# First stage of a two-block transformer kernel: late modulation sums dealt anew, modulation units in pairs, columns by transposes, latent queries rotated first

## The reference, cut to what matters

```
mod   = silu(c)     @ w_ada + b_ada      # 6 parts of 2048 columns: sh_a, sc_a, gt_a, sh_f, sc_f, gt_f
mod_c = silu(c_ctx) @ w_ada + b_ada      # only sh_a, sc_a are used
h  = rms_norm(x)   * (1 + sc_a)  + sh_a  # 256 latent tokens
hc = rms_norm(ctx) * (1 + csc_a) + csh_a # 256 context tokens
h @ w_in, hc @ w_in                      # 4928 columns, feeding four kinds of attention
```

## Time and profile before

| | us |
|---|---|
| median of 3 runs | 2803.4 (2800.49 to 2805.45) |
| the profiled execution | 2806.29 |
| its span | 2804.3 |
| PE busy | 2735.3 (98%) |
| DVE busy | 1696.7 (61%) |
| ACT busy | 1165.0 (42%) |
| POOL busy | 197.2 (7%) |
| DMA read over the span | 205 GB/s |

### The profile page before, as it was taken

The page is one execution under the profiler, slowest core; times in us unless marked ns, Lnnn a source line. Parts: engine busy times, 40 slices in busy tenths (PEclk is TensorE's granted clock), DMA queues, the critical chain, the costliest instruction groups (busy, mean ns, idle before and its releaser), DMA issues.

```text
span 2804.3 us, 32889 instructions
## 1 busy us (share of the span) xinstructions
PE 2735.3 (98%) x12547; PEld 2224.0 (79%) x12547; DVE 1696.7 (61%) x2039; ACT 1165.0 (42%) x1520; POOL 197.2 (7%) x219
## 2 busy tenths in 40 slices
PE   5999999999999999999999999999999999999998
PEld 2587877687888888888888888888888888888887
DVE  2378974766466666655574566554565655656566
ACT  3222224544444444444454444444444443444444
POOL 0024404101000000000040000000000000000000
PEclk9999999999999999999999999999999999999999
DMA  9988873246666677555555544655565656556563
GB/s 346 346 278 306 305 281 113 76 180 207 212 209 226 239 245 245 195 185 192 180 210 195 169 146 139 222 195 195 180 196 192 188 189 194 180 184 192 192 194 120
DMA packets 285788, 577.48 MB, mean 206 GB/s; under 512 B 13986, under 2 KB 18562, under 8 KB 283646
## 3 DMA queue, kind: packets, MB, share of 16 engines
q1 hardware_dynamic: 276936, 542.05, 57.9%
q0 software_dynamic: 6752, 31.14, 3.1%
q10 hardware_dynamic: 2006, 3.02, 0.3%
HBM read 571.04 MB, written 5.14 MB: 205 GB/s over the span
## 4 chain that ended last, share of the span: by engine, by line
PE 87%; issue 4%; DVE 4%; DMA 3%; POOL 1%; POOLq 1%; ACT 0%; DVEq 0%; SPq 0%; ACTq 0%
PE bank L384 27%; PE bank L386 26%; PE bank L385 26%; DMA w_raw<-in_w_ada 3%; PE bank L2021 1%; DVE proj_x L1677 1%; PE bank L667 1%; DVE w_lo L380 1%; PE bank L984 1%; PE bank L488 1%; PE bank L831 0%; PE bank L693 0%; PE bank L868 0%; PE bank L616 0%; PE bank L669 0%
## 5 line engine op out<-in xcount | busy, mean ns | idle before, releaser
L380 DVE TENSOR_TENSOR w_lo<-w_raw,w_hi 128x1024 fp32r<-128x1024 f32 (+1 forms) x848 | 1030.8, 1237 | 568.3 <-ACT w_hi L372 566.3
L372 ACT ACTIVATE w_hi<-w_raw 128x1024 fp32r<-128x1024 f32 (+1 forms) x848 | 880.9, 1054 | 1158.3 <-PE bank L386 994.1
L384 PE MATMUL bank<-w_hi,xa_hi 128*128 128x512 f32 (+1 forms) x2272 | 894.4, 394 | 10.0 <-DVE w_lo L380 10.0
L386 PE MATMUL bank<-w_hi,xa_lo 128*128 128x512 f32 (+1 forms) x2272 | 884.7, 389 | 0.0
L385 PE MATMUL bank<-w_lo,xa_hi 128*128 128x512 f32 (+1 forms) x2272 | 884.5, 389 | 0.0
L384 PEld LDWEIGHTS bank<-w_hi,xa_hi 128*128 128x128 f32 x2272 | 428.6, 189 | 109.8 <-issue 19.9
L386 PEld LDWEIGHTS bank<-w_hi,xa_lo 128*128 128x128 f32 x2272 | 428.2, 188 | 89.1
L385 PEld LDWEIGHTS bank<-w_lo,xa_hi 128*128 128x128 f32 x2272 | 428.6, 189 | 86.0
L384 PE MATMUL bank<-w_hi,ffn_act_hi 128*128 128x512 f32 x800 | 311.4, 389 | 0.0
L386 PE MATMUL bank<-w_hi,ffn_act_lo 128*128 128x512 f32 x800 | 311.3, 389 | 0.0
L385 PE MATMUL bank<-w_lo,ffn_act_hi 128*128 128x512 f32 x800 | 311.2, 389 | 0.0
(11 more groups left out here) (321 smaller groups left out, 1816.7 us busy)
## 6 DMA issues: line engine op xcount, KB each, us to landing
w_raw<-in_w_in SPq DMA_DIRECT2D x116, 1024.0 KB, 5.1
w_raw<-in_w_ada SPq DMA_DIRECT2D x80, 1024.0 KB, 7.3
w_raw<-in_w_up SPq DMA_DIRECT2D x64, 1024.0 KB, 5.7
w_raw<-in_w_down SPq DMA_DIRECT2D x64, 1024.0 KB, 5.0
w_raw<-in_ffn_wg SPq DMA_DIRECT2D x44, 1024.0 KB, 5.2
w_raw<-in_ffn_wu SPq DMA_DIRECT2D x44, 1024.0 KB, 5.2
w_raw<-in_ffn_wd SPq DMA_DIRECT2D x44, 1024.0 KB, 5.1
w_raw<-in_w_out SPq DMA_DIRECT2D x32, 1024.0 KB, 5.1
```

Source lines behind the costliest of these rows:

```text
L372: act.activation(whi[:, slot, ks, 0:w], raw[:, q, ks, 0:w], ACT.Copy)\
L380: dve.tensor_tensor(wlo[:, slot, ks, 0:w], raw[:, q, ks, 0:w], whi[:, slot, ks, 0:w].bitcast(F32), ALU.subtract).then_inc(sem("lo_made"), 1)
L384: pe.matmul(out, xh, wh, start=first, stop=False)
L386: return pe.matmul(out, xl, wh, start=False, stop=last)
```

## The change

- SP's five small loads at the start (c, c_ctx, g_attn, b_ada, identity) move to ACT's queue.
- Four late tiles, `LATE_AHEAD` (sums 2 and 3, k = 0 and 1), are loaded at the end of `FRONT` and summed by DVE right behind the last `h_lo`; the other 44 are dealt anew by `BY_VECTOR`, sums 4v+2 and 4v+3 ahead of 4v and 4v+1.
- At i = 1 DVE makes the sums before the two copies.
- The rows of b_ada for the late parts are loaded from ACT's queue in groups 1 and 2 of the front, instead of from SP behind the fourth load of the mixed stage.
- In the front, modulation units run in pairs with the pieces behind each pair; a chunk's columns come behind the pieces; columns are four transposes, and DVE reduces them.
- The folds of v = 0 and 1 come one unit later than the old rule would put them.
- POOL rotates the latent queries between the two halves of the grouped queries; the first copies into `probsT` wait for the second half.

```diff
-U_OUT = U_MIX + 4 * (len(WIN) - 2) + 4 * N_LATE_D + 4
+U_OUT = U_MIX + 4 * (len(WIN) - 2) + 4 * N_LATE_D
+LATE_AHEAD = [(2, 0), (3, 0), (2, 1), (3, 1)]
 def front_loads():
-    return loads
+    return loads + [("late", a, k) for a, k in LATE_AHEAD]
-BY_VECTOR = {2: (0, 2, 2, 4), 3: (0, 2, 0, 2), 4: (2, 2, 2, 2), 5: (2, 2, 2, 2), 6: (2, 2, 2, 4), 7: (4, 2, 4, 0)}
+BY_VECTOR = {2: (2, 2, 2, 2), 3: (0, 2, 0, 0), 4: (2, 2, 4, 2), 5: (2, 2, 2, 2), 6: (2, 2, 4, 2), 7: (2, 2, 2, 0)}
-    queue = [(a + s, k) for a in range(0, N_LATE_D, 2) for k in range(4) for s in range(2)]
+    queue = [(a + s, k) for v in range(3) for a in (4 * v + 2, 4 * v) for k in range(4) for s in range(2)]
+    queue = [tile for tile in queue if tile not in LATE_AHEAD]
-FOLD_AT = [min(i for i, n in enumerate(W) if n > LAST_SUM[v] and MIX[n][2] >= 1) for v in range(3)]
+FOLD_AT = [min(i for i, n in enumerate(W) if W[i - (v < 2)] > LAST_SUM[v] and MIX[n][2] >= 1) for v in range(3)]
 def front_read(sp, n):
+                elif kind == "late":
+                    sp.wait_ge(sem("sum_step"), 8 * q + 8)
 # act, where the first pair of probabilities is copied; dve the same
+                if s["d"] == 0:
+                    act.wait_ge(sem("rotated_pe"), 2)
 # sync: the five small loads leave, to the head of the scalar engine's program
-            sp.dma_start(crow[0:16, :], ...)
...
-                if n == 3:
-                    late_b_piece(0)
-                    late_b_piece(1)
 # scalar, in the loop over g
+                if g in (1, 2):
+                    for b in range(4):
+                        col = 2 * D + (4 * (g - 1) + b) * NCH
+                        act.dma_start(late_rows[g - 1][32 * b:32 * b + 32, :], ...)
 # vector: take(c)
-                cols = ps[4 + c % 2][:, 0:8].rearrange("p (k v) -> p k v", v=2)
+                cols = ps[4 + c % 2][:, :].rearrange("p (k j v r) -> p k v r j", k=4, j=4, v=2)[:, :, :, 0, :]
+                dve.tensor_reduce((s_col if c % 2 == 0 else b_col)[:, k, :], cols, AX.X, ALU.add)
+                dve.drain()
 # vector, behind the loop over g
+            multiply_ahead(0)
+            multiply_ahead(1)
+            def late_pairs(i):
+                for first in range(W[i] + 1, W[i] + 1 + FOLLOW[i], 2):
+                    multiply((first, first + 1))
 # vector, the loop over W
                 if i == 1:
+                    late_pairs(i)
                     win_copy(0)
                     win_copy(1)
+                    continue
                 if i >= 2:
                     behind(i - 2)
-                for first in range(n + 1, n + 1 + FOLLOW[i], 2):
-                    multiply((first, first + 1))
+                late_pairs(i)
 # tensor: columns(c)
-                    m = pe.matmul(ps[4 + c % 2][:, 2 * k:2 * k + 2], rows_1[:, c % 2, k * P:k * P + P], pick[:, :], ...)
+                    m = pe.transpose(ps[4 + c % 2][:, k * P:k * P + P], rows_1[:, c % 2, k * P:k * P + P], ident[:, :])
 # tensor: the loop over g
-                rest = list(PIECES[g])
-                for u in range(8):
-                    c, q = 2 * g + 2 + u // 4, u % 4
-                    ada_unit(c, q)
-                    if u < 5:
-                        w, j = rest.pop(0)
-                        early_piece(pe, w, g, j)
-                    if q == 3:
-                        columns(c)
-                for w, j in rest:
+                c = 2 * g + 2
+                for u in range(0, 8, 2):
+                    ada_unit(c + u // 4, u % 4)
+                    ada_unit(c + u // 4, u % 4 + 1)
+                    for w, j in (PIECES[g][0:2], PIECES[g][2:4], PIECES[g][4:5], PIECES[g][5:6])[u // 2]:
+                        early_piece(pe, w, g, j)
+                    if u % 4 == 2:
+                        columns(c + u // 4)
+                for w, j in PIECES[g][6:8]:
                     early_piece(pe, w, g, j)
 # gpsimd
             copied(8)
-            for i in range(2):
-                (norm and rope of the grouped queries of token tile i)
+            gqa_queries(0)
             (wait for mla_copied; rope of the latent queries)
             pool.drain().then_inc(sem("rotated_pe"), 1)
+            gqa_queries(1)
+            pool.drain().then_inc(sem("rotated_pe"), 1)
```

More of the change, by code:

```diff
@@ L413, in early_hi, with early_lo @@
                     .then_inc(sem("early_hi"), 1)
-        def early_lo(dve, w, g):
+        def early_lo(dve, w, g, halves=(0, 1)):
             q = FRONT.index(("win", w, g)) % 4
-            for h in range(2):
+            for h in halves:
                 dve.wait_ge(sem("early_hi"), 4 * g + (1 if w == 1 else 3) + h)
@@ L817, in att1_dve @@
                 wait(dve, "att_out", s["d"] - 1)
+                if s["d"] == 0:
+                    dve.wait_ge(sem("rotated_pe"), 2)
                 pt_copy(dve.tensor_copy, s, 1).then_inc(sem("att_pt_copied_d"), 1)
@@ L1296, in _ @@
         def _(sp):
[L1297 to L1302, removed]
             for i in range(4):
@@ L1313, in _ @@
                 front_read(sp, n)
-                src = w_ada_v[:, q, :, ada_cols(c)] if kind == "ada" else w_in_v[:, q, :, WIN[c][0]:WIN[c][0] + NCH]
+                if kind == "late":
+                    src = w_ada_v[:, q, :, 2 * D + c * NCH:2 * D + (c + 1) * NCH]
+                else:
+                    src = w_ada_v[:, q, :, ada_cols(c)] if kind == "ada" else w_in_v[:, q, :, WIN[c][0]:WIN[c][0] + NCH]
                 sp.dma_start(raw[:, n % 4, :, :], src).then_inc(sem(f"landed{n % 4}"), 16)
@@ L1389, in _ @@
         def _(act):
+            act.dma_start(crow[0:16, :], t["c"].rearrange("a (k p) -> (a k) p", p=P)).then_inc(sem("c_loaded"), 16)
+            act.dma_start(crow[16:32, :], t["c_ctx"].rearrange("(k p) -> k p", p=P)).then_inc(sem("c_loaded"), 16)
+            act.dma_start(csig[32:48, :], t["g_attn"].rearrange("a (k p) -> (a k) p", p=P)).then_inc(sem("consts_loaded"), 16)
+            act.dma_start(csig[48:80, :], t["b_ada"][:, 0:2 * D].rearrange("a (k p) -> (a k) p", p=P))\
+                .then_inc(sem("consts_loaded"), 16)
+            act.dma_start(ident[:, :], t["identity"]).then_inc(sem("consts_loaded"), 16)
             act.wait_ge(sem("memsets"), 2)
@@ L1421, in _ @@
                 h_hi(act, g, 1)
+                if g in (1, 2):
+                    for b in range(4):
+                        col = 2 * D + (4 * (g - 1) + b) * NCH
+                        act.dma_start(late_rows[g - 1][32 * b:32 * b + 32, :],
+                                      t["b_ada"][:, col:col + NCH].to_broadcast([32, NCH])).then_inc(sem(f"b_loaded{g - 1}"), 16)
             def win_copy(c):
@@ L1636, in _ @@
             dve.drain()
-            dve.scalar_tensor_tensor(g_one_b[:, :], small_cols[:, 2, :], 1.0, small_cols[:, 0, :], ALU.add, ALU.mult)
-            dve.tensor_reduce(pick[:, :], ident[:, :].rearrange("p (j v r) -> p v r j", j=4, v=2)[:, :, 0, :], AX.X, ALU.add).then_inc(sem("c_spread"), 1)
+            dve.scalar_tensor_tensor(g_one_b[:, :], small_cols[:, 2, :], 1.0, small_cols[:, 0, :], ALU.add, ALU.mult)\
+                .then_inc(sem("c_spread"), 1)
             def spread2(cols):
@@ L1684, in multiply, with multiply_ahead @@
                             reached[c] = ("lo_made", 2 * u + 2)
+            def multiply_ahead(k):
+                for j in range(KQ):
+                    for a in (2, 3):
+                        n = FRONT.index(("late", a, k))
+                        if j == 0:
+                            dve.wait_ge(sem(f"landed{n % 4}"), 16 * (n // 4) + 16)
+                        w, cj, acc = raw[:, n % 4, j, :], ccol[:, 4 * k + j:4 * k + j + 1], late_sums(a)
+                        if k == 0 and j == 0:
+                            m = dve.tensor_scalar(acc, w, cj, None, ALU.mult)
+                        else:
+                            dve.wait_ge(sem("sum_step"), reached[a][1])
+                            m = dve.scalar_tensor_tensor(acc, w, cj, acc, ALU.mult, ALU.add)
+                        m.then_inc(sem("sum_step"), 1)
+                        steps[0] += 1
+                        reached[a] = ("sum_step", steps[0])
             def add_rows(v):
@@ L2028, in columns @@
                 for k in range(4):
-                    m = pe.matmul(ps[4 + c % 2][:, 2 * k:2 * k + 2], rows_1[:, c % 2, k * P:k * P + P], pick[:, :],
-                                  start=True, stop=True)
+                    m = pe.transpose(ps[4 + c % 2][:, k * P:k * P + P], rows_1[:, c % 2, k * P:k * P + P], ident[:, :])
                 m.then_inc(sem("ada_columns"), 1)
@@ L2310, in _ @@
                      sin128[:, i, :], 64, 4)
+            copied(8)
+            gqa_queries(0)
             pool.wait_ge(sem("mla_copied_a"), 1)
```

9 lines of the change are left out of this document (4 added, 5 removed).

## The result

The changed kernel takes 2810.2 us (median of 22 runs, 2806.5 to 2812.7) against 2804.3 (22 runs, 2800.5 to 2808.7): a ratio of 1.0018, 95% interval 1.0011 to 1.0024. It is slower, by 5.9 us in the medians (5 us by the ratio), where 0.9 us less was forecast. The forecast time, 2802.5, is 7.7 us too low; the range (2793 to 2811) holds the result. What follows compares places in the traces.

What follows compares the result with a forecast made beforehand. PE was taken to bound the kernel nearly everywhere. Terms -2.5+17.6+1.9-10.8-3.7-3.4 = -0.9 took the profiled 2806.3 to 2805.4 us, and 2.9 less for the median gave 2802.5; range 2793 to 2811.

Steps and rivals of the forecast that it cites:

- The front: Stage up to 158.04 us: start, columns, groups and end together -2.5 us, with three groups of 29.3 us counted +0.5.
- L+13.5: Front's ring: second projection tile is free 13.5 us after L, the last modulation tile's landing; before it was 11.9.
- The start: Kernel start: first x load leaves at 0.74 instead of 3.05, so -2.3 us; bounds 0 and -2.3.
- Columns by transposes: Front: four transposes replace eight selector instructions, DVE reduces more; net -0.25 us on the path per chunk.
- The end of the front: From the start of the last columns to the front's end: 24.2 us instead of 25.5, so -1.3.
- The new wait: Before PE's first mixed-stage unit: idle 17.6 us for DVE's copy of projection 0, plus 1.9 of low clock.
- T+31.1: Mixed stage: DVE's copy of projection 0 is done 31.1 us after T, the end of the last h_lo.
- The mixed stage: Behind the new wait: PE's idle times before projections 3 and 4 and last fold go, -10.8 us, and -3.7 of clock.
- The queries: Near 462 us: POOL's flag comes earlier, 1.90 us idle and 1.5 of low clock go, -3.4.
- (a): Rival: bias-row spread eats the lead, PE waits before projection 3 again, +6.5+2.0, total 2811 us; chance 0.23.
- (b): Rival: stall only 12.3 us and the ring does not bind, groups of 27.8 us, total 2793; chance 0.19.
- (c): Rival: copy of projection 0 does not hold PE, so no stall, 17.6+1.9 go, total 2783 us; chance 0.05.

Runs made afterwards that it cites:

- e1: Changed kernel with the front's modulation units and pieces in the order of before, columns still by transposes; 2805.4 us.
- g3: Kernel before with small loads on ACT's queue, columns by transposes, latent queries first, plus the change's pairs; 2804.7 us.
- f3: Kernel before with the small loads on ACT's queue, columns by transposes and latent queries first; 2799.9 us.
- f4: Kernel before with the columns by transposes only; 2804.4 us.
- e4: Kernel before with only the latent queries rotated between the halves of the grouped queries; 2802.9 us.
- f1: Changed kernel with the old unit order and, on both engines, each early projection copied behind its own unit, ahead of that unit's sums; 2800.8 us.
- g2: Kernel of f1 with another deal of the late tiles (BY_VECTOR), projections 2 to 7; 2795.9 us (7 runs).
- e2: Changed kernel, units in pairs, with the odd chunk's columns ahead of the piece; 2805.1 us.
- f2: Kernel of f1 with two late tiles fewer behind projection 2's first unit and two more behind projection 5's third; 2799.1 us.

## Why the prediction was wrong, point by point

- **The front, the step that failed** ("Start, groups and end: -2.3-0.25+0.5-1.3", rounded to -2.5): it came as +0.6. The loop through the ring was seen, but the old loop was said to lie "under PE's own 28 to 29", so that pairs would cost 0.5 us in all. They cost 4.8 (e1, g3).
  - *The new loop's size.* "L+13.5" for the second projection tile was right: in the group of the rows above the last unit of the group before (the second of the two at 98.60) starts at 99.53 and the split is done at 110.54 + 2.36 = 112.90, 13.4 later. The next load into that buffer is used at 118.12, 5.2 later, as priced. The "four more at 2.7 us each" then took until 130.34, 12.2 us instead of 10.8: the first two behind the hold came 3.4 us apart. With that a group is 13.4 + 5.2 + 12.2 = 30.8, not 29.3. From last unit to last unit the three groups take 28.5 (40.67 to 69.13), 30.4 and 30.8 us: the first is as long as in the old order, as no piece stands ahead of the columns at 42.45 that open it.
  - *The old loop's size.* 28.5 (f3, f4), not 27.8; PE waits 1.2 to 1.3 us there for the last load of the last two groups. The mean of 29.3 in before hides three unequal groups, 28.7, 31.1 and 28.1 us, as two rows of before show beside the 44.68 and 132.53 of the earlier trace rows. In the second, 3.3 us were lost to a low clock at 73 to 81 us (0.57), which other executions have less of (e4: 0.79). At full clock PE and the ring were level, so PE's own saving could win nothing, and 29.3 as the measure of "nothing changes" was a poor base.

```profile
73.34 1.49 PE L2029 MATMUL bank<-row_pick,ada_rows 128*128 128x2 f32 x8 [0.72 <-ACT ada_rows L1407]
104.44 1.05 PE L2029 MATMUL bank<-row_pick,ada_rows 128*128 128x2 f32 x8 [0.72 <-ACT ada_rows L1407]
```

  - *The piece counted once too few.* The groups were priced from landing to landing, and the end from the start of the last columns. The step between them, from 1.8 to 3.9 us because the piece stands there, is in neither: +2.1.
- **The start, -2.3:** the first modulation product comes at 21.84 instead of 23.06, -1.2, though SP's first x load does leave at 0.74. The ten kernels with the small loads on ACT's queue have it at 20.9 to 22.0, mean 21.4, the three with them on SP's (before, e4, f4) at 22.4 to 23.1, mean 22.8: -1.5. By the first odd columns the gain is larger, 1.8 us (means of 42.6 and 44.3), and 2.2 in the two traces compared. The far end of 0 and -2.3 was chosen, and the truth lay between, near that end for the sum. Why the first load comes only half as much earlier was not tried.
- **Columns by transposes, -0.25 a chunk:** the three groups together became 0.8 (against e4) to 2.1 us (against before) shorter, where -0.25 for six chunks is 1.5. The size fits by luck: all of it lies in the one group whose clock had been low, and the groups at full clock gained nothing (f4).
- **The end of the front, -1.3:** from the last columns to the start of the last product 158.41 - 134.20 = 24.2 us, against 157.81 - 132.53 = 25.3: -1.1, right.
- **The new wait, 17.6 us and T+31.1:** 17.35, and the copy done at 175.90, which is T+31.05 with T = 144.85. Both waits for loads are there (2.79 and 2.52 us). The term from the trace's 5.06 us a load holds. By the estimate from the Trainium skill (DMA: Bandwidth & Descriptors, Anatomy of one DMA), 4.4 us, the stall would have been 16.3. That section gives its two terms for DMAs that GpSimd issues, and these loads are SyncE's; the measurement decides against the estimate here. The clock behind it cost 2.5 us, not 1.9.
- **The mixed stage, -10.8 and -3.7:** count from where the front's last product would make room for the next, 0.23 us behind its start (158.04 before, 158.64 after). To the latent keys the kernel before needed 304.6 us, after needs 308.9, so +4.3. Take from it the 17.5 us to PE's next product (176.16) and 2.5 of clock, and add the 1.55 us less at the keys: -14.2 against -14.5. Right to half a us, with a new 0.96 at 296.08 in it.
- **The queries, -3.4:** between 462 and 474 us the distance between the traces shrinks from 4.9 to 3.3, and the idle time from 1.90 to 0.35: -3.2. Whether it lasts to the end, e4 leaves open.
- **Sum:** of the 7.7 us by which the time was missed 3.1 are the front, about 1.1 the clock, the idle time of the mixed stage and the 0.35 left at the keys, and 0.9 the distance between the profiled execution and the median (2.0 over 22 runs instead of 2.9 over three). 2.6 us remain between the places of one pair of traces (3.3 us apart at 474 us) and the medians (5.9): they are not explained. The front alone turns the forecast of -0.9 into +2.2; it is the largest term that was missed, not the whole of the miss.
- **The rivals.** (a), the gaps stay, gave nearly the measured time, 2811, for a reason that did not happen. (b) and (c) did not happen. What did, the ring held by the piece, stood in the forecast itself, at +0.5 for three groups, and in no rival; the far bound of the groups (+3) had another reason, the low clock.
- **The signs.** Of those that the prediction named, the stall of 15 to 20 us, the 32 sums with two waits for loads, the missing idle times before projections 3 and 4 and the missing wait for POOL all came. Only the columns of the last chunk did not: 134.20 instead of 130 to 131. Groups that are too long stood under no sign of being wrong.

Taken together: start, transposes and queries -4.6 (f3); pairs +4.8 (e1, g3); four tiles ahead, the new deal and all else that f1 has and f3 has not +0.9 (f1 against f3), and the sums ahead of the copies +4.6 (e1 against f1): +5.7, and +5.9 is measured. The four steps lead from before to the changed kernel by way of f3, f1 and e1, so their sum has to come out and is no proof by itself; the pairs' +4.8 is confirmed apart from it, by g3 against f3. The folds, the earlier copies and the bias rows on ACT's queue are in the +0.9 and were not tried alone. Whether the four tiles ahead are a gain is not shown: g2 has them, with each copy behind its own unit and another deal, but no kernel has that deal without them.

## What to carry to other kernels

Price a loop through a ring from one event back to the same event, and lay the path that leaves the loop from that event too; a step between two reference points is otherwise in neither sum. When PE seems to bound a stage whose loads run all the time, look whether the loop of the loads is as long, and look at each turn and its clock, not at the mean: making PE cheaper then gives nothing (f4), and work put ahead of what frees a buffer costs most of its length in every turn (2.7 us of products, 1.8 to 2.2 us a group). A stall at a stage's border is partly paid back where the next stage is bound by another engine: shorten it and move that engine's work as well; here the first gave 4.6 of 16.1 us (f1), and the second another 4.8 (g2).

## What the runs showed of the hardware

Loads that run back to back came 2.7 us apart (1 MB each); behind a hold of the ring, where SP stood up to 8.5 us, the next two came 3.4 us apart (118.12 to 124.92). DMA throughput within the last group of the front was 355 GB/s in the changed kernel and 372 in e2, with the columns first. The two rows:

```profile
103.00:134.00 31.00, 26.68 (x147) 15.51 (x146) 10.38 (x19) 7.31 (x10) 0.00 (x0) 1.00 0.99 355
```

```profile
103.00:130.00 27.00, 24.31 (x136) 13.66 (x135) 8.82 (x14) 5.49 (x7) 0.00 (x0) 1.00 1.05 372
```

From 45 us on, PE's granted clock was at its lower level for some 3 to 7 us behind every idle time of 3.4 us or more in these traces, and about 1.5 to 3 us of work were lost in each such stretch. Behind idle times of 1.9 to 2.7 us it fell in some cases (2.68 us at 219.42 in before) and not in others (1.94 us at 118.12 in the changed kernel). It also fell with no idle time over 1 us ahead: at 493 to 501 us in four of the eleven kernels that no longer have the pause at 462 us (e4, f1, f2, g3), and not in the others.
